# Attention stages: TensorE turns the next step's weights ahead of turning the last step's output back

## The reference, cut to what matters

```python
def block(c):                         # 128 queries at a time
    s = jnp.einsum('bqhd,bkhd->bhqk', qb, k) * scale
    mask = kpos[None, :] <= (s0 + jnp.arange(ATTN_BLOCK))[:, None]
    p = _masked_softmax(s, mask)
    return jnp.einsum('bhqk,bkhd->bqhd', p.astype(v.dtype), v)
```

## The kernel before, in words

| engine | order in iteration n |
|---|---|
| TensorE | scores(n+2), back(n-1), turn(n+1), values(n) |
| ScalarE | take(n+1), exps(n+2), lift(n), what runs beside |
| VectorE | maxima(n+2), take(n+1), inverses(n), output(n-1), what runs beside |

## Time and profile before

### The profile page before, as it was taken

The page is one execution under the profiler, slowest core; times in us unless marked ns, Lnnn a source line. Parts: engine busy times, 40 slices in busy tenths (PEclk is TensorE's granted clock), DMA queues, the critical chain, the costliest instruction groups (busy, mean ns, idle before and its releaser), DMA issues. The chain is left out here.

```text
span 2772.6 us, 56650 instructions
## 1 busy us (share of the span) xinstructions
PE 2584.4 (93%) x21595; PEld 1752.1 (63%) x21596; DVE 1361.9 (49%) x3120; ACT 753.3 (27%) x1652; POOL 298.7 (11%) x448
## 2 busy tenths in 40 slices
PE   6998889899998879999979999999999999999998
PEld 6977674334433324443448667888888766888887
DVE  2236744444443434544465785544344687544333
ACT  4235530000000000000023565422233366433222
POOL 4111002222221212222210000000000000000000
PEclk8998999999999989999989999999999999999999
DMA  7254159999999999899983300233223210222221
GB/s 228 82 196 144 73 238 391 420 419 407 419 419 406 414 419 409 334 418 418 416 327 122 118 2 11 89 111 109 91 91 100 98 54 2 69 92 99 92 101 51
DMA packets 171288, 589.13 MB, mean 212 GB/s; under 512 B 28270, under 2 KB 55726, under 8 KB 121912
## 3 DMA queue, kind: packets, MB, share of 16 engines
q1 hardware_dynamic: 158544, 563.70, 51.9%
q0 software_dynamic: 10160, 18.02, 1.9%
q10 hardware_dynamic: 2360, 4.29, 0.4%
HBM read 574.26 MB, written 17.45 MB: 213 GB/s over the span
## 5 line engine op out<-in xcount | busy, mean ns | idle before, releaser
L2774 PE MATMUL moe_up<-expert_w,mod 128*32 128x512 f32 x3200 | 393.4, 617 | 54.6 <-DMA expert_w<-in_exp_w_up 30.6
L2839 ACT ACTIVATE mod<-mod 128x256 f32<-128x256 f32 x85 | 35.6, 418 | 966.1 <-DVE mod L2875 946.3
L2774 PEld LDWEIGHTS moe_up<-expert_w,mod 128*32 128x32 f32 x3200 | 114.9, 112 | 283.3 <-issue 208.9
L2774 PE MATMUL moe_up<-ring,mod 128*32 128x512 f32 x1784 | 221.1, 616 | 24.2 <-DMA ring<-in_exp_w_up 19.5
L423 ACT ACTIVATE feed_w<-ring 128x1024 fp32r<-128x1024 f32 (+1 forms) x160 | 153.8, 1036 | 263.6 <-PE feed_bank L370 263.6
L2783 PE MATMUL moe_down<-expert_w,mod 128*32 128x256 f32 x3568 | 215.2, 384 | 1.7 <-DVE mod L2886 1.7
L368 PE MATMUL feed_bank<-feed_w,mlp_u_hi 128*128 128x512 f32 x512 | 199.3, 389 | 0.0
L370 PE MATMUL feed_bank<-feed_w,mlp_u_lo 128*128 128x512 f32 x512 | 199.2, 389 | 0.0
L369 PE MATMUL feed_bank<-feed_w,mlp_u_hi 128*128 128x512 f32 x512 | 199.2, 389 | 0.0
L2783 PEld LDWEIGHTS moe_down<-expert_w,mod 128*32 128x32 f32 x3568 | 134.1, 112 | 93.2 <-issue 39.8
L437 DVE TENSOR_TENSOR feed_w<-ring,feed_w 128x1024 fp32r<-128x1024 f32 (+1 forms) x160 | 185.4, 1221 | 13.2 <-ACT feed_w L423 12.9
(11 more groups left out here) (556 smaller groups left out, 4992.4 us busy)
## 6 DMA issues: line engine op xcount, KB each, us to landing
expert_w<-in_exp_w_up SPq DMA_DIRECT2D x153, 1024.0 KB, 10.4
expert_w<-in_exp_w_down SPq DMA_DIRECT2D x83, 1024.0 KB, 10.3
ring<-in_exp_w_up SPq DMA_DIRECT2D x80, 1024.0 KB, 10.4
ring<-in_w_ff SPq DMA_DIRECT2D x32, 2048.0 KB, 8.5
ring<-in_exp_w_down SPq DMA_DIRECT2D x32, 1024.0 KB, 10.1
ring<-in_ada_w SPq DMA_DIRECT2D x12, 2048.0 KB, 12.0
x<-in_exp_w_up SPq DMA_DIRECT2D x23, 1024.0 KB, 10.5
x<-in_exp_w_down SPq DMA_DIRECT2D x13, 1024.0 KB, 10.3
```

The costliest lines, as they stand in the source:

```text
L2774: mm = nc.tensor.matmul(up[quarter[q], :], rowsT[:, c, :], w[:, q], start=(c == 0), stop=(c == UPS - 1))
L2839: nc.scalar.activation(sig, gate, ACT.Sigmoid, scale=ALPHA).then_inc(sig_ready, 1)
```

## The change

In TensorE's list `turn(n+1)` is put ahead of `back(n-1)`. Nothing is added or removed; the other engines' lists and all waits stay as they are.

```diff
             for n in range(n_steps):
                 if n + 2 < n_steps:
                     scores(n + 2)
+                if n + 1 < n_steps:
+                    turn(n + 1)
                 if n >= 1:
                     back(n - 1)
-                if n + 1 < n_steps:
-                    turn(n + 1)
                 values(n)
             back(n_steps - 1)
```

## The result

The changed kernel ran at 2755.34 us (median of 5, 2752.39 to 2762.45) beside 2771.19 (2769.41 to 2772.84) before: ratio 0.9937, 95% interval 0.9918 to 0.9955. A second set, on another chip, gave 0.9942 (0.9929 to 0.9956).

The account below looks back on a forecast made before the run. A TensorE-ScalarE round trip was taken to bound sparse steps, TensorE the latent ones. 2 x (7.9 sparse + 0.6 stage end) + 3.8 mix, less 0.8, gives 20 us: 2771.2 - 20 = 2751.2 us, range 2746 to 2761.

Parts of the forecast that it names:

- The mechanism: Attention stages: turn(n+1) no longer stands behind back's wait for the lift, so TensorE and ScalarE stop waiting for each other.
- the round trip: Sparse steps: ScalarE's take waits for turns, TensorE's back for the lift, once a step; 3.08 us in the wide step.
- TensorE's joints in the sparse steps: Gaps between TensorE's pieces, taken as about 0.4 us a step, 0.06 of it between scores and what follows.
- The tie between engines: Rival: TensorE, VectorE and the scores-to-values path lie within 0.1 us; gain only 10 to 14, 2757 to 2761; chance 0.25.
- the table of the larger need: Sparse steps: per iteration the larger of TensorE's and VectorE's needs; sums 16.8 and 16.5, larger 17.2 in eight steps.
- the wait of the take for the turns: Sign in eight sparse steps: ScalarE's wait for turned weights falls from 6.0 us to below 2.
- The end of a stage: Last step but one: turns go in back's 1.29 wait for the lift, values start earlier; 0.6 us a layer.
- Mix: Mix stage: VectorE's recorded waits for TensorE, 5.8 us, shrink; gain 3.8, bounds 2 and 5.8.
- Is it kept: Behind the three stages: what follows each starts when it ends, so all of the gain counts as kept.
- The sum: Whole kernel: 2 x (7.9 + 0.6) + 3.8 = 20.8, less 0.8 for near ties: 20 us.
- TensorE alone binds: Rival in the sparse steps: VectorE's work slides past by a step; gain 25 us, 2746; chance 0.12.
- The clock: Rival in the attention stages: granted clock falls, eight steps take 11 us more, two such windows eat the gain; chance 0.02.

Follow-up runs that it names:

- mix alone: Kernel before with the new order of turn(n+1) and back(n-1) in the mix stage only: 2768.96 us beside 2772.51, ratio 0.9981.
- att alone: Kernel before with the new order in stages att0 and att1 only, mix in the old order: 2757.96 us, ratio 0.9950.
- two edits of opposite sign: Changed kernel with sparse scores over all 128 rows (2775.42 us); changed kernel with back(n-1) behind values(n) (2762.01 us, ratio 0.9968).

## Why the prediction was right, and which term was off

*The mechanism* was right. Back's wait is gone, the latent steps stand still (21.04, said 21.06), mix fell on the stretch named to 49.78 (said 50), no wait of output for `back` has come, and the granted clock stays at 1.00 in all three stages. The lift moved ahead in ScalarE's list shows the round trip from the other side.

*The mis-sized term* is TensorE's joints in the sparse steps, as the prediction put it: "I take 0.06 more between scores and what follows, for which no step shows a case without a wait". That joint is 0.21, and the turn behind it 0.06 longer. TensorE's need in eight steps was given as 16.8; with 0.15 more a step it is 18.0, and 17.93 was measured, with TensorE full. So the steps gave 1.56 per eight and not 2.27. Over the 28 intervals that is 5.3 a layer (66.71 us from the first to the 29th `back` before, 61.45 after), said 7.9. In the sparse steps before, the joint lay inside `back`'s wait for the lift, in every one. The latent joints of 0.12 (scores 1.98 long from 1669.44, `back` at 1671.26: 1.82, less 1.71 of issue) are twice what I took. And the very case stood in the mix stage of the trace of before, with scores on 64 rows too:

```profile
311.40 1.13 PE L1115 MATMUL mix_s<-qk 64*128 64x512 f32 x4
...
311.80 0.26 ACT L1189 ACTIVATE mix_heads<-mix_o 128x128 f32<-128x128 f32 x1
...
312.46 0.33 PE L1145 MATMUL mix_o<-ident,mix_heads 128*128 128x128 f32 x1
```

The lift is over at 312.06, 0.40 ahead of `back`, so `back` does not wait for it. It starts 1.06 after the scores of 4 groups, less 0.85 of issue: 0.21, and it lasts 0.33 itself. So the prediction was wrong that no step shows this case, and the term could have been sized before the change. The run with the sparse scores over all 128 rows shows to what it belongs.

*The tie between engines*, for which I took off 0.8 and which as a rival had a chance of 0.25, did not happen: without the gates VectorE has 1.27 less to do and nothing moves. The gain of 16.8 lies between what that rival forecast (10 to 14) and the forecast's own 17 to 23, so the time alone would not have told them apart. In one thing the table of the larger need was wrong for the same reason: it had VectorE bind four of eight steps; TensorE binds all.

*A sign that missed* is the wait of the take for the turns: 4.3, said below 2. The prediction had the take follow the lift at once, 0.18 after its start; in the wide step it starts 0.88 after it (1604.75 to 1605.63), because TensorE is the engine that comes last. The eight sparse steps, too, lie outside the 17.0 to 17.6 that were named.

*The end of a stage* gave 1.3 (the last three intervals 7.57 before, 6.25 after) and its beginning took 0.4 back (the first `back` now stands behind turn(1), 7.7 after the first scores in place of 7.3): 0.9 net, said 0.6.

*Mix* gave 4.4, said 3.8. *Is it kept:* the sum of the stages is 16.8, the runs say 15.9 and 18.6 by their medians; what was won in the att stages is kept, as the stretches behind them (536.9 and 415.4) did not grow. Behind mix the scatter of 7.5 us leaves open how much is kept; mix alone gave a ratio of 0.9965 to 0.9997.

*The sum* came near by some luck. The joints took 2 x 2.6 = 5.2 from the 20 us, and smaller misses gave 2.0 back: 0.6 at the ends of the stages, 0.6 in mix, and the 0.8 taken off for a tie that was not there.

*TensorE alone binds*, the rival with 0.12, is what the sparse steps show; with the joints as they are it gives not 25 but 17 us.

*The clock* did not fall in the changed kernel: nine transposes in a row, and 1.00 throughout. The Trainium skill ("TensorE: Matmul & The Clock Gate", Part 4: PE-mode transpose), which the prediction set beside this rival, says that the full clock doesn't engage for transposes. The measurement is otherwise: behind att0 it rises among transposes alone (rows in the last section). The clock can fall in mix with the old order, though, as the trace of att alone shows, and it cost 1.2 us there; the prediction saw no ground for a fall and gave 0.02.

The Trainium skill has a rule that bears on the joint: "TensorEngine Tiling (Array Packing)", Key Properties, says that a change of the tiling mode drains TensorE. This case's traces agree: one passage a step between tiled and whole-array work costs 0.15 us, in two edits of opposite sign (one fewer: 8 x 0.15 less; one more: 8 x 0.15 more).

## What to carry to other kernels

When two engines wait for each other once a step, look for work that is ready in the list behind the waiting instruction and put it ahead; the gain ends where the next engine is full, and that engine's need has to be summed with the joints between its pieces. A joint that lies inside a wait can't be read there. Look through the other stages of the same trace for the same pair of pieces without a wait, above all where tiled and whole-array matmuls meet; only where there is none, take the nearest pair, and the size of the gap as a bound.

## What the runs showed of the hardware

- Passing from fp32 scores on two 64-row tiles to transposes costs 0.21 us and makes the first transpose 0.06 longer (0.33); from scores on 96 or 128 rows it costs 0.12, with no longer transpose (0.27).
- Two fp32 score matmuls on 64-row tiles take 0.213 us for each group of 128 keys together, over 128 rows 0.427 (0.63 to 0.85 from 2 to 3 groups; 0.55 to 0.97 from 1 to 2 groups over 128 rows). So the tiles pay here even with one group, as their passage costs 0.15.
- The granted clock can fall from 1.00 to 0.50 inside a stage that keeps 1.00 in other traces of the same code, after 5.4 us in which TensorE was busy for 3.81 in either case (the trace of att alone).
- The clock does rise on transposes alone. Behind att0 TensorE runs 64 transposes (L709) and nothing else; in the changed kernel the granted clock goes from 0.50 (1.2 GHz) to 1.00 (2.4 GHz) among them, 32 taking 6.70 and the next 16 1.95:

```profile
1687.00:1690.00 3.00, 3.00 (x15) 3.00 (x16) 1.36 (x6) 2.94 (x7) 0.00 (x0) 0.50 0.55 175
...
1693.00:1695.00 2.00, 2.00 (x21) 2.00 (x20) 2.00 (x4) 2.00 (x4) 0.00 (x0) 1.00 0.00 0
```

```profile
1686.79 6.70 PE L709 MATMUL feed_bank<-tok,nsa_o 128*128 128x128 f32 x32 [2.02 <-PEq L2944]
1693.32 1.95 PE L709 MATMUL feed_bank<-tok 128*128 128x128 f32 x16
1695.10 1.95 PE L709 MATMUL feed_turn<-tok 128*128 128x128 f32 x16
```
